# Moving one routing step, its transposes and four row dot products in a fused transformer kernel

## The reference

```python
def one(xb):                                   # a chunk of tokens
    q = (xb @ wq).reshape(C, PEER_HEADS, 2, PEER_DK_HALF)
    s = jnp.einsum('chpd,hpnd->chpn', q, keys)           # 8 heads, 2 x 128 keys
    sv, si = lax.top_k(s, K)                             # K = 16 of 128, twice
    cand = sv[:, :, 0, :, None] + sv[:, :, 1, None, :]
    top_s, sel = lax.top_k(cand.reshape(C, PEER_HEADS, K * K), K)
    eidx = ...                                           # 128 experts of 16384 per token
    g = jax.nn.softmax(top_s, axis=-1)
    u = u_tab[eidx]
    act = jax.nn.gelu(jnp.einsum('chkd,cd->chk', u, xb), approximate=False)
    w = g * act
    return jnp.einsum('chk,chkd->cd', w, v_tab[eidx])
```

## Time and profile before

| | |
|---|---|
| median of three runs | 2084.07 us |
| the profiled execution | 2084.11 us |
| its span | 2082.3 us |
| TensorE busy | 2059.0 us, 99% |
| VectorE, ScalarE, GpSimd busy | 1435.4, 1006.2, 1022.5 us |
| part one of the schedule, tile 1 | about 363 to 438 us of the span |
| rounds 1 and 2 | about 438 to 628 us |

### The profile page before, as it was taken

How to read it: one execution, slowest core, us unless ns; L and a number is a source line. 1 busy time by engine, 2 the same in 40 slices (tenths; PEclk the granted TensorE clock), 3 DMA queues, 4 the chain that set the end, 5 groups by cost and what they waited for, 6 DMA issues and landing times.

```text
span 2082.3 us, 31695 instructions
## 1 busy us (share of the span) xinstructions
PE 2059.0 (99%) x11823; PEld 1848.4 (89%) x11823; DVE 1435.4 (69%) x2792; ACT 1006.2 (48%) x1843; POOL 1022.5 (49%) x582
## 2 busy tenths in 40 slices
PE   9999999999999999999999999999999999999998
PEld 8746889999999999999999999999967777877777
DVE  6247547989997467878778788877687535057763
ACT  4337433368888743333333333333546652356643
POOL 3212456764445566665666766564344444411242
PEclk9999999999999999999999999999999999999999
DMA  5330225767677899999899999996322223210021
GB/s 202 80 99 11 82 81 167 240 214 267 233 245 287 301 338 341 332 348 358 321 335 358 334 336 350 335 342 233 111 87 74 82 92 111 100 41 31 21 81 61
DMA packets 145752, 419.68 MB, mean 202 GB/s; under 512 B 13376, under 2 KB 60096, under 8 KB 143808
## 3 DMA queue, kind: packets, MB, share of 16 engines
q1 hardware_dynamic: 108736, 283.42, 39.5%
q0 software_dynamic: 36864, 134.23, 17.5%
HBM read 375.06 MB, written 42.53 MB: 201 GB/s over the span
## 4 chain that ended last, share of the span: by engine, by line
PE 94%; DVE 3%; issue 1%; ACT 1%; DMA 1%; SPq 0%; POOL 0%; DVEq 0%; ACTq 0%
PE bank L502 20%; PE bank L503 19%; PE bank L504 19%; PE bank L908 5%; PE bank L909 5%; PE bank L910 5%; PE bank L889 4%; PE bank L1117 2%; PE bank L677 1%; PE wide L1140 1%; PE wide L1128 1%; PE bank L1140 1%; PE wide L635 1%; PE bank L771 1%; PE bank L772 1%
## 5 line engine op out<-in xcount | busy, mean ns | idle before, releaser
L2638 POOL TENSOR_TENSOR wl<-wraw,wh 128x1024 fp32r<-128x1024 f32 x272 | 679.7, 2503 | 792.2 <-ACT wh L1303 791.2
L1303 ACT CAST wh<-wraw 128x1024 fp32r<-128x1024 f32 x360 | 376.2, 1046 | 198.0 <-PE bank L504 163.0
L502 PE MATMUL bank<-XH,wh 128*128 128x384 f32 (+2 forms) x976 | 347.7, 356 | 1.2 <-ACT wh L1303 1.2
L503 PE MATMUL bank<-XL,wh 128*128 128x384 f32 (+2 forms) x976 | 344.5, 353 | 0.0
L502 PE MATMUL bank<-WTH,wh 128*128 128x384 f32 x1024 | 343.1, 335 | 0.6 <-issue 0.4
L504 PE MATMUL bank<-WTH,wl 128*128 128x384 f32 x1024 | 342.7, 335 | 0.0
L504 PE MATMUL bank<-XH,wl 128*128 128x384 f32 (+2 forms) x976 | 342.6, 351 | 0.0
L503 PE MATMUL bank<-WTL,wh 128*128 128x384 f32 x1024 | 342.4, 334 | 0.0
L502 PEld LDWEIGHTS bank<-XH,wh 128*128 128x128 f32 x976 | 183.3, 188 | 23.3 <-issue 4.6
L908 PE MATMUL bank<-XH,wh 128*128 128x384 f32 x576 | 199.8, 347 | 0.3 <-issue 0.3
L503 PEld LDWEIGHTS bank<-XL,wh 128*128 128x128 f32 x976 | 183.3, 188 | 18.5 <-issue 2.2
(11 more groups left out here) (536 smaller groups left out, 3787.9 us busy)
## 6 DMA issues: line engine op xcount, KB each, us to landing
wraw<-in_wstream SPq DMA_DIRECT2D x360, 512.0 KB, 4.5
g_scratch<-gs SPq DMA_DIRECT2D x12, 2048.0 KB, 7.4
gr<-g_scratch SPq DMA_DIRECT2D x15, 1536.0 KB, 13.6
a_scratch<-tmp SPq DMA_DIRECT2D x72, 192.0 KB, 2.3
tmp<-a_scratch SPq DMA_DIRECT2D x46, 192.0 KB, 7.1
sq<-a_scratch SPq DMA_DIRECT2D x26, 192.0 KB, 9.5
shifted<-hc_scratch SPq DMA_DIRECT2D x12, 270.0 KB, 4.8
h<-in_hT SPq DMA_DIRECT2D x8, 264.0 KB, 6.9
```

The lines of the kernel that those rows point to most:

```text
L502: pe.matmul(o, w1, x1, start=n == 0, stop=False)
L503: pe.matmul(o, w1, x2, start=False, stop=False)
L1303: act.copy(wh[n % NSPLIT][:, :], wraw[n % NRAW][:, :]).then_inc(*w_hi.tell(n))
L2638: return pool.tensor_tensor(lo, src, hi.bitcast(F32), ALU.subtract)
```

## The change

Five edits, all in this schedule:

- TensorE's generator of `route` has one more `yield` ahead of the transposes, and ScalarE's one more ahead of the copy to `ijgT`.
- Part one picks four rows more: in step 2, and a second one in steps 8, 10 and 12.
- Rounds 1 and 2 pick six rows each where they picked eight.
- Rounds 1 and 2 hand out the 26 chunks of the routing over 14 steps where it was 15.
- The step-15 part of a product that TensorE runs ahead is capped at the end of a product.

```diff
@@ tensor: route
                 mm.then_inc(*key_mm.tell((tt, half)))
                 for _ in range(5):
                     yield
-            for _ in range(15):
+            for _ in range(16):
                 yield
@@ drive_routing
                 spill()
-                if tt == 1 and n > 2:
+                if tt == 1 and n > 1:
                     pick()
+                    if n in (8, 10, 12):
+                        pick()
                 if tt == 1 and n % 3 == 2:
                     spill()
             for _ in steps:
                 pass
-        picks = 10
+        picks = 14
@@
                     if ahead:
-                        ahead(KT * base + KT * count * 31 // 32)
+                        ahead(min(KT * base + KT * count * 31 // 32, KT * spilled[0] + KT - 1))
@@
-                while picks < (10, 18, 26)[tt - 1] + (8, 8, 16)[tt - 1] * (n + 1) // 16:
+                while picks < (14, 20, 26)[tt - 1] + (6, 6, 16)[tt - 1] * (n + 1) // 16:
                     pick()
                     picks += 1
-                while done < ROUTE_STEPS * (n + 1) // 15:
+                while done < ROUTE_STEPS * (n + 1) // 14:
                     next(steps, None)
@@ scalar: route
             act.activation(gates, gates, ACT.Exp).then_inc(*gate_exp.tell(tt))
-            for _ in range(2):
+            for _ in range(3):
                 yield
```

## The result

The changed kernel takes 2087.47 us, the kernel before 2084.01 us (medians of 20 runs each). The ratio of the runs is 1.0014, with a 95% interval of 1.0008 to 1.0020: 2.9 us slower (1.7 to 4.2). The two medians lie 3.5 us apart; the text goes by the ratio. I had forecast 2083.5 us, a hair faster. Two later comparisons of the same kernels gave 1.0010 (1.0001 to 1.0019) and 1.0018 (1.0009 to 1.0027). The profiled execution took 2086.37 us, 1.1 us under the median.

The account below looks back on a forecast made before the run. TensorE, busy 2059.0 of 2082.3 us, was the bound, so only its waits and clock could count. The terms -1.1, -0.3, -1.7, +2.1 and +0.4 gave -0.6 us, so 2083.5 us; 8-in-10 range 2079.8 to 2087.8.

Parts of the forecast that it names:

- The exponential a step earlier: Rounds 1 and 2, TensorE's waits at L880 for ScalarE's Gelu: shorter by 1.1 us and 0.3 us.
- The clock: Round 2, behind the wait at L880: the stretch at 1.2 GHz goes, -1.7 us; called the least certain term.
- The transposes of tile 1: Part one: these transposes run a product later, about 438.1 us; cost 0 if the first scatter stays in time.
- The cover of 1.2 us: Part one: the first token is ready at 440.9 us, TensorE's first scatter starts at 442.14, leaving 1.2 us.
- Four more rows in part one: Part one: added rows delay GpSimd's split, so TensorE waits 2.1 us at the product of 433.93; bounds 0 and 5.8.
- milder form: Part one: rows of step 12 land late and the one-hots start 2 us late, over the 1.2 us to spare.
- my slow rival: Part one becomes the bound: GpSimd falls behind, TensorE waits 5.8 us; +4.8 us, 2088.9 us; chance 0.18.
- Step 10 of the rounds: Round 2's late split: VectorE runs about 1.05 us later there, +0.4 us; bounds -0.5 and +1.05.
- the two picks fewer in rounds 1 and 2: Rounds 1 and 2: nothing of TensorE waits for a picked row, so fewer picks change the time by 0.
- The rule against the trace: By the skill's rule a dot product costs a GpSimd fetch nothing; a fetch held 1.9 us beside L2245 disagreed.
- the rival that rested on it: Part one: GpSimd catches up, added dot products cost it nothing, the 2.1 us wait goes; 2081.4 us, chance 0.20.
- the waits at L880 go entirely: Rounds 1 and 2: both waits vanish, -3.84 - 1.7 = -5.5 us, so 2078.6 us; chance 0.10.

Follow-up runs that it names:

- exp_early: The kernel before with ScalarE's exponential of rounds 1 and 2 and its two table loads two chunks earlier, nothing else moved; ratio 1.0019 (1.0010 to 1.0028).

## Why the prediction was wrong

- **What bounds the kernel** held: every difference in the stage is a wait of TensorE or its clock.
- **The exponential a step earlier**: in round 1 -1.1 us and a wait of 0.8, measured -1.0 and 0.83 in all three traces of the change. That was right in mechanism and size. In round 2 the wait fell to 0.83, not to 1.6, and the scatter ahead of it took 0.5 us more, so the net is -0.6 where -0.3 stood: near, but partly by luck. What I said beside it, that VectorE has its gates in time in either place, holds in the change and fell in exp_early.
- **The clock, -1.7 us: the first step that failed.** I let the stretch go with the wait of 1.9 us behind which it stood, and did not ask whether the change makes new waits. In the stage, over 17 traces, a stretch came behind 8 of the 15 waits of 1.9 us and more, and behind no shorter one; each of the two traces of before has one. The change removes both old waits and makes new ones, of 2.6 us near 607 in each of its three traces and of 2.3 at the first scatter in one; behind two of these four stands a stretch (1.6 us each). One per trace became two in three traces, too few to tell from no change. So the runs show no gain in the place of -1.7.
- **The transposes of tile 1**: 0, and 0.0 with ten rows. The cover of 1.2 us fell short only through VectorE's rows.
- **Four more rows in part one, +2.1**: measured 0.5 to 4.8 us in six traces, 2.3 in the mean and 2.0 without the stretch at 1.2 GHz in one of them; +2.0 (0.9 either way) in time against kernels that lose some 0.8 us in round 3. The size was right, and in that there is luck: the waits that I named, of products for late splits, are 0 to 1.1 us in all. The rest is the first scatter, by the "milder form" of my slow rival: a late row, held by two splits in a row, ahead of the one-hots. I had put it at one side of a rival with 0.18; it came in four traces of six.
- **Step 10 of the rounds, +0.4, and "the two picks fewer in rounds 1 and 2 ... both 0": the second step that failed, and the larger.** Nothing of TensorE waits for a picked row, that is true, but the weight split waits behind the picked row's fetch, and for the operation of VectorE that its dot product pushes back. With six rows one falls into step 10 of round 2, ahead of the split that was already the late one, and with the faster routing it meets L2247. Measured +2.3 us in each of three traces, outside my bound of +1.05, and 2.2 (0.9 either way) in time for the row; the kernels without that row lose 0.4 us there, which is what I had priced. For part one I had worked out just this price (a fetch held once, 2.82 us in place of 0.95); I didn't look where the remaining rows of the rounds would fall.
- **The rule against the trace**: the fetch of 2.76 us beside L2247, and one of 2.75 at 422.59 beside the same operation, repeat what the earlier trace rows showed. The rule that descriptor generation passes beside an operation with two SBUF inputs (the Trainium skill, "SBUF — State Buffer", "Who interferes with whom") doesn't hold for these fetches, and the rival that rested on it fell.
- **The rival "the waits at L880 go entirely"** has a slip in its sum: -5.5 leaves out the +2.1 and +0.4 of the other terms, with which it comes to 2081.1 us and not 2078.6.

Put together: -1.0 (round 1), -0.6 (L880 of round 2), +2.0 (part one), +2.3 (the product near 607) and +0.4 (two small gaps, near 613 and 619 us) give +3.1, with the clock at nothing; measured +2.9. Of the 3.7 us between this sum and the forecast's -0.6 the clock is 1.7 and round 2 near 607 to 619 us is 2.3; the other terms take 0.3 off. The range of 8 in 10, 2079.8 to 2087.8, holds the median of 2087.5, but the forecast had the wrong sign, and my own mark of failure, over 2087 us, was passed by that median.

## What to carry to other kernels

An instruction that nobody waits for still has a price, that of its place: read what stands behind it in its queue, for the rows that a change leaves alone in number but moves in place too. Where two engines exclude each other, 0.1 to 0.3 us in their starts decides which of two is held for the whole length of the other, so take such operations out of the steps in which a deadline stands, and test a schedule over several executions. A wait removed by moving work on one engine is a gain only once the next releaser's slack is read: in exp_early one held dot product was enough to use it up.

## What the runs showed of the hardware

- VectorE and GpSimd exclude each other for short operations too: L2267, a 128x128 multiplication of 0.29 us, took 2.38 us beside a split, and the custom operation L2233 2.35 in place of 0.29 us. The one-hots `hots` and the reductions L2254 were never held in this stage; in the changed kernel's first trace those of 604 to 609 us ran beside the split of 605.18 in their usual time. The changed kernel, 400 to 730 us, durations in ns (min/median/max) of each:

```profile
L2289 DVE TENSOR_TENSOR hots<-wide,ijgT x48: 1208/1217/1257, 439.6 to 698.0; 128x1024 f32<-128x1024 f32 x48
```

```profile
L2254 DVE TENSOR_REDUCE ijg<-spare x6: 2276/2282/2286, 414.4 to 613.4; 128x128 f32<-128x2048 uint32 x6
```

- In this stage the granted clock fell to about half (1.2 GHz) behind 8 of 15 waits of 1.9 us or more, and behind none shorter: seven times for 3.4 us, 1.5 to 1.6 us lost, and once for 6.8 us, 2.8 us lost (behind the wait of 2.86 us). Which of two equal waits it follows changes from one execution of the same kernel to the next. It is no rule for other places: near 1540 us nine of the 17 traces have such a stretch, where the longest wait in the 30 us ahead of it is 0.72 us.
- Of two fetches held equally long (2.76 us, rounds 1 and 2 of one trace) one cost TensorE nothing and the other was part of a gap of 2.6 us.
- A single trace of one kernel can differ by 2 us from the next of the same kernel far behind the place of a change (weights that land late near 1103 to 1111 us); so the sum over the stage of the change has to be read, not the difference of two spans.
